# Differential attention on one core: join factors for two heads at once, and the join placed between the two sides' minima

## Chip, core and metric

The kernel runs on one core of a Trainium2 chip. The metric is the device time of one execution in microseconds (us), lower is better. The median of three executions before the change is 2317.76 us (2317.54 to 2319.17).

## What is computed

Three layers on a sequence of 1024 tokens of width 1024: a gated block with a convolution and a feed-forward part, then a layer of differential attention, then a layer of stick-breaking attention. The change touches the differential attention alone. Cut to what matters:

```python
def block(args):                       # i = 0..7, 128 query rows each
    i, qb1, qb2 = args
    mask = kpos[None, :] <= qpos[:, None]
    def probs(qb, k):
        s = jnp.einsum('bhqd,bshd->bhqs', qb, k).astype(jnp.float32) * scale
        return jax.nn.softmax(jnp.where(mask, s, -jnp.inf), axis=-1)
    a = probs(qb1, k1) - lam * probs(qb2, k2)
    return jnp.einsum('bhqs,bshe->bhqe', a.astype(v.dtype), v)
...
o = _rms(o, subln) * (1.0 - lambda_init)
o = o.reshape(b, s, DA_V) * jax.nn.silu(g)
return x + o @ w_out
```

There are 8 heads. Each has two sides (q1, k1 and q2, k2) whose softmaxes are subtracted.

## The kernel before

The program is written by hand, one instruction stream for each engine (functions `tensor`, `vector`, `scalar`, `gpsimd`, `sync`), with semaphores between them. Every engine executes its own stream strictly in order, so the order of the calls in the source is the order of the work. Small helpers at the head of the file issue every instruction, so that the profile names a helper's line: L72 is a matmul, L75 a transpose, L81 an activation, L84 a copy on ScalarE, L93 a `tensor_tensor`, L101 a `scalar_tensor_tensor`, L104 the fused minimum over a row (`tensor_tensor_reduce`), L110 a `tensor_reduce`, L113 a reciprocal.

**Groups.** `da_groups` (line 489) cuts the attention into N = 54 groups: row block 0 in two groups of 4 heads, block 1 in four groups of 2 heads, blocks 2 to 7 in eight groups of one head each. A group of block i has `width(i)` = 128 (i + 1) key columns a head. `da_first` = 22 is the first group of block 4: from there on a side has its own pair of PSUM banks, and three such pairs go round. "Five blocks", "eight blocks" are widths of 640 and 1024 columns: groups 22 to 29 have five, 30 to 37 six, 38 to 45 seven, 46 to 53 eight.

**What a group u passes through.** TensorE: `scores(u)`, both sides with the mask added, into PSUM; the banks of group u + 1 come free with the exponential of side 0 of group u. VectorE: `top(u, sides)`, the negated maximum of each row (called a minimum below), for both sides in one instruction up to group 21 and one side after the other from 22 on. ScalarE: `exp(u, 0)` and `exp(u, 1)`, which also write each row's sum. VectorE: the join. A reciprocal of side 1's sum and a small multiply with side 0's sum and lambda give a factor (both write `oss`, one column for a head), and one `scalar_tensor_tensor` over the whole width adds side 1 times its factor into side 0. TensorE: `turn_a`, transposes of the joined rows in halves of 512 columns, all through PSUM bank 6. ScalarE: `turned`, the copy of each half into one of two buffers. TensorE: the product with the values, four heads into bank 7. When four heads (a quartet) are done, ScalarE squares the bank and VectorE multiplies it with the gate (L93, 128x512) and sums the squares (L110).

**Order before.** One loop over u on each engine:

- TensorE (line 977): scores(u); transposes of u - 2, first half; product of u - 3; transposes of u - 2, second half.
- VectorE (line 1955): top(u); from group 22 on side 0, then side 1; factors and join of u - 1, which wait for exp(u - 1, 1); multiply and sum where u - 3 closes a quartet; then, in a few rounds from u = 27 to 38, pieces of other work (peaks of the gate, the factor of weight 31, the factor of the output).
- ScalarE (line 2678): exp(u, 0); copy of u - 2, second half; the square where u - 3 closes a quartet; exp(u, 1); for u = 22 to 29 the absolute sum of an eighth of weight 31 (an activation of 128x512 into OV); copy of u - 1, first half.
- GpSimd takes maxima across partitions for weights; SyncE's queue loads the weights in order. Its load of weight 31 waits for the transposes of group 3 and the join of group 2, since it overwrites their buffers.

At u = N VectorE takes the reciprocal of the norm's roots for the first four row blocks and scales them (`finish_half`, 8 times, then `finish_low`), ScalarE takes the root (`finish_root`, which needs another activation table), and TensorE transposes them (`finish_turn`) in its last round, before and behind the last product. The output projection follows.

The first exponentials are interrupted on ScalarE at u = 2 by the last two SiLU pieces, between two table loads.

Of the kernel before, what the change touches and what calls it, by code (L numbers as in the profile page):

```python
# [200 lines left out]
def block_kernel(nc, A):  # L201
    ctx = ExitStack()
    with ctx:
# [359 lines left out]
        def tensor(e):  # L563
# [413 lines left out]
            for u in range(2, N + 3):  # L977
# [4 lines left out]
                turn_a(u - 2, 0)  # L982
                if u == N + 2:
                    for i in range(4):
                        finish_turn(i, 0, i)
                if u >= 3:
                    v = u - 3
                    i, hs = da_groups[v]
                    for x, h in enumerate(hs):
                        if h % 4 == 0:  # L990
                            banks.take_at(("pva", i, h // 4), 7)
                            e.wait_ge(*banks.free(("pva", i, h // 4)))
                            e.wait_ge(*sig("bank_act").at("vv", 1, NT - 1))
                        bo = banks.ap(("pva", i, h // 4))
                        for j in range(i + 1):
                            at = width(i) * x + 128 * j
                            e.wait_ge(*sig("turned_a").at(v, at // 512))
                            mm = e.matmul(bo[:, 128 * (h % 4):128 * (h % 4) + 128], AT[v % 2][:, at:at + 128],
                                          VV[:, j, 128 * h:128 * h + 128], start=(j == 0), stop=(j == i))
                    mm.then_inc(*full.up("pva", i, hs[-1]))  # L1000
                turn_a(u - 2, 1)
                if u == N + 2:
                    for i in range(4):
                        finish_turn(i, 1, (i + 4) % 6)
# [156 lines left out]
        def vector(e):  # L1161
# [793 lines left out]
            for u in range(N + 4):  # L1955
                if u < da_first:
                    top(u, (0, 1))
                elif u < N:
                    top(u, (0,))
                    top(u, (1,))  # L1960
                if 1 <= u < N + 1:
                    v = u - 1
                    i, hs = da_groups[v]
                    w, n = width(i), len(hs)
                    a, a2 = ea(v), e2(v)
                    ri, ro = oss[:, 8 * (v % 2):8 * (v % 2) + n], oss[:, 8 * (v % 2) + 4:8 * (v % 2) + 4 + n]
                    e.wait_ge(*sig("exp").at(v, 1))
                    e.reciprocal(ri, l_sum(1, i, hs[0], n)).then_inc(*step.up())
                    e.wait_ge(*step.last())
                    e.scalar_tensor_tensor(ro, l_sum(0, i, hs[0], n), lamt[:, 5:6], ri, ALU.mult,  # L1970
                                           ALU.mult).then_inc(*step.up())
                    e.wait_ge(*step.last())
                    for x in range(n):
                        ax = a[:, w * x:w * x + w]
                        join = e.scalar_tensor_tensor(ax, a2[:, w * x:w * x + w], ro[:, x:x + 1], ax, ALU.mult, ALU.add)
                    join.then_inc(*sig("joined_a").up(v))
                if 3 <= u < N + 3 and da_groups[u - 3][1][-1] % 4 == 3:
                    i, hs = da_groups[u - 3]
# [27 lines left out]
                if u == N:  # L2006
# [174 lines left out]
        def scalar(e):  # L2181
# [496 lines left out]
            for u in range(N + 4):  # L2678
# [6 lines left out]
                turned(u - 2, 1)  # L2685
                if 3 <= u < N + 3 and da_groups[u - 3][1][-1] % 4 == 3:
                    i, hs = da_groups[u - 3]
# [15 lines left out]
                if u == 2:  # L2703
# [3 lines left out]
                    turned(0, 0)  # L2707
                if u >= 2:
                    turned(u - 1, 0)
                for x in {N + 1: range(4), N + 2: range(4, 8)}.get(u, ()):  # L2710
# [418 lines left out]
```

## Time and profile before

| | |
|---|---|
| median of three executions | 2317.76 us (2317.54 to 2319.17) |
| the profiled execution's own time | 2321.46 us |
| its span | 2319.7 us |
| TensorE busy | 2256.5 us, 97% |
| VectorE busy | 1512.9 us, 65% |
| ScalarE busy | 951.3 us, 41% |
| GpSimd busy | 202.8 us, 9% |
| granted clock of TensorE | 0.998 of full speed |
| the chain that ended last | TensorE 86%, VectorE 8%, ScalarE 4% |

The profile is one execution, and its span is what all views are measured in, from 0 to 2319.7 us. PE is TensorE, DVE VectorE, ACT ScalarE, POOL GpSimd, SP SyncE. Busy time is the time within instructions; a busy TensorE need not be at its peak. The first attention is a small part of the span, between about 1338 and 1562 us. A line's buffer names are those of the program without their numbers: PS is PSUM, RG holds the exponentials of both sides, OV and RG the transposed copies, mx the minima, oss the join's factors, R the gate.

### The profile page before, as it was taken

How to read it: one execution, taken by the hardware profiler on the slowest of the kernel's cores; microseconds unless marked ns; L12 is line 12 of the kernel's file. 1: busy time of each engine (PE TensorE's matmuls, PEld its weight loads, DVE VectorE, ACT ScalarE, POOL GpSimd, SP SyncE). 2: the span in 40 equal slices, each digit the busy share in tenths (PEclk: the TensorE clock that was granted, in tenths of full speed). 3: DMA queues.
4: the chain of work that ended last, by engine and by line, in shares of the span. 5: the costliest groups of instructions: out<-in, count | busy, mean ns of one | idle time of the engine just before them, and what ended most of it. 6: DMA issues, size and time to landing. Idle time of an engine off the chain costs nothing.

```text
span 2319.7 us, 29678 instructions
## 1 busy us (share of the span) xinstructions
PE 2256.5 (97%) x12574; PEld 1153.8 (50%) x12574; DVE 1512.9 (65%) x1959; ACT 951.3 (41%) x1396; POOL 202.8 (9%) x246
## 2 busy tenths in 40 slices
PE   7999999999999999999999988899999999999999
PEld 5455444444444444444544446664444444566655
DVE  6789857866766766778653268995553460677761
ACT  6255234423232323342332178772322321677750
POOL 0001021000000000352320200002100000000000
PEclk9999999999999999999999999999999999999999
DMA  5111110121112111112122010011032140001021
GB/s 193 37 37 37 37 37 21 53 73 70 39 37 73 62 48 70 40 39 110 37 73 73 1 37 1 1 73 63 11 104 114 51 132 1 1 1 37 2 92 55
DMA packets 51972, 120.16 MB, mean 52 GB/s; under 512 B 2890, under 2 KB 8579, under 8 KB 51456
## 3 DMA queue, kind: packets, MB, share of 16 engines
q1 hardware_dynamic: 48616, 105.40, 12.8%
q10 hardware_dynamic: 3224, 12.87, 1.6%
q8 instruction: 99, 1.62, 0.3%
q14 instruction: 33, 0.27, 0.0%
HBM read 101.49 MB, written 12.58 MB: 49 GB/s over the span
## 4 chain that ended last, share of the span: by engine, by line
PE 86%; DVE 8%; ACT 4%; DMA 1%; issue 1%; SPq 0%; DVEq 0%; ACTq 0%
PE PS L72 80%; PE PS L75 5%; ACT RG L81 2%; DVE R L93 2%; DVE R L101 1%; DVE RG L104 1%; DVE RG L101 1%; DMA RG<-in_a_w_in 1%; ACT R L81 1%; DVE oss L110 1%; DVE dg L104 1%; DVE scl L110 0%; DVE mx L110 0%; ACT OV L81 0%; DMA R<-in_x 0%
## 5 line engine op out<-in xcount | busy, mean ns | idle before, releaser
L72 PE MATMUL PS<-R,RG 128*128 128x512 f16 (+1 forms) x5568 | 1186.0, 374 | 9.2 <-DVE R L101 4.2
L72 PEld LDWEIGHTS PS<-R,RG 128*128 128x128 f16 (+1 forms) x5568 | 550.3, 103 | 637.5 <-issue 11.0
L72 PE MATMUL PS<-RG,R 128*128 128x512 f16 (+2 forms) x3080 | 601.1, 361 | 0.9 <-DVE R L93 0.5
L72 PEld LDWEIGHTS PS<-RG,R 128*128 128x128 f16 (+1 forms) x3080 | 279.3, 105 | 297.5 <-issue 15.6
L81 ACT ACTIVATE RG<-RG,scl 128x4096 f16<-128x4096 f32 (+2 forms) x70 | 177.8, 2556 | 206.8 <-DVE scl L113 206.8
L101 DVE SCALAR_TENSOR_TENSOR RG<-RG,scl 128x4096 f16<-128x4096 f32 (+2 forms) x70 | 213.0, 3050 | 71.0 <-ACT RG L81 71.0
L107 DVE TENSOR_TENSOR_SCAN RG<-RG,dg 128x128 f32<-128x128 f32 (+7 forms) x128 | 167.6, 1347 | 123.2 <-ACT RG L81 122.7
L101 DVE SCALAR_TENSOR_TENSOR R<-PS,scl,R 128x512 f32<-128x512 f32 (+1 forms) x211 | 148.5, 742 | 114.0 <-PE PS L72 107.4
L110 DVE TENSOR_REDUCE scl<-RG 128x1 f32<-128x4096 f32 (+1 forms) x35 | 150.3, 4294 | 99.8 <-DMA RG<-in_w_ff 41.2
L81 ACT ACTIVATE R<-PS,scl 128x512 f32<-128x512 f32 (+1 forms) x104 | 68.6, 686 | 265.3 <-PE PS L72 251.7
L122 POOL PARTITION_ALL_REDUCE scl<-scl x49 | 33.9, 694 | 1592.1 <-DVE scl L110 1311.2
L72 PE MATMUL PS<-R 64*128 64x512 f16 (+4 forms) x1216 | 142.7, 338 | 18.3 <-ACT RG L81 18.0
L75 PE MATMUL PS<-ident,RG 128*128 128x128 f32 x864 | 146.9, 285 | 10.1 <-DVE RG L101 7.3
L81 ACT ACTIVATE R<-R,scl 128x512 f16<-128x512 f32 (+3 forms) x68 | 79.3, 1193 | 135.4 <-DVE R L93 78.0
L101 DVE SCALAR_TENSOR_TENSOR R<-R,OV 128x1024 f32<-128x1024 f32 x104 | 129.3, 1278 | 1.0
L81 ACT ACTIVATE RG<-PS,scl 128x1024 f32<-128x1024 f32 (+4 forms) x94 | 89.0, 948 | 81.7 <-PE PS L72 81.7
L75 PEld LDWEIGHTS PS<-ident,RG 128*128 128x128 f32 x864 | 92.3, 141 | 48.4 <-issue 32.7
L81 ACT ACTIVATE RG<-PS,mx,scl 128x128 f32<-128x128 f32 (+7 forms) x128 | 106.1, 833 | 11.1 <-DVE mx L104 9.8
L93 DVE TENSOR_TENSOR R<-PS,R 128x512 f32<-128x512 f32 (+1 forms) x120 | 80.9, 685 | 44.0 <-PE PS L72 29.5
L84 ACT COPY R<-PS 128x512 f32<-128x512 f32 x72 | 40.9, 581 | 144.7 <-PE PS L75 74.2
L72 PEld LDWEIGHTS PS<-R 64*128 64x128 f16 (+1 forms) x1216 | 59.4, 99 | 79.1 <-ACT RG L81 24.8
L93 POOL TENSOR_TENSOR R<-R 128x512 f32<-128x512 f32 x56 | 86.1, 1554 | 133.2 <-ACT R L81 117.9
(141 smaller groups left out, 1675.0 us busy)
## 6 DMA issues: line engine op xcount, KB each, us to landing
RG<-in_w_ff SPq DMA_DIRECT2D x16, 2048.0 KB, 8.5
RG<-in_a_w_in SPq DMA_DIRECT2D x8, 2048.0 KB, 8.7
xspill<-R ACTq DMA_DIRECT2D x2, 4096.0 KB, 15.8
RG<-in_w_kv SPq DMA_DIRECT2D x4, 2048.0 KB, 7.9
RG<-in_b_w_in SPq DMA_DIRECT2D x4, 2048.0 KB, 8.4
RG<-in_w_in SPq DMA_DIRECT2D x3, 2048.0 KB, 8.4
R<-in_x SPq DMA_DIRECT2D x8, 512.0 KB, 8.6
RG<-in_w_out SPq DMA_DIRECT2D x2, 2048.0 KB, 7.7
```

Source lines behind the costliest of these rows:

```text
L72: return self.engine.matmul(*a, **k) if self.engine else Nothing()
L75: return self.engine.transpose(*a) if self.engine else Nothing()
L81: return self.engine.activation(*a, **k) if self.engine else Nothing()
L84: return self.engine.copy(*a) if self.engine else Nothing()
L93: return self.engine.tensor_tensor(*a) if self.engine else Nothing()
L101: return self.engine.scalar_tensor_tensor(out=out, in0=in0, scalar=scalar, in1=in1, op0=op0, op1=op1)
L104: return self.engine.tensor_tensor_reduce(*a) if self.engine else Nothing()
L107: return self.engine.tensor_tensor_scan(*a) if self.engine else Nothing()
L110: return self.engine.tensor_reduce(*a, **k) if self.engine else Nothing()
L122: return self.engine.partition_all_reduce(*a) if self.engine else Nothing()
```

## The change

On VectorE the join of group u - 1 behind both minima becomes the join of group u - 2 between the two minima (behind the one minimum up to group 21). The factors of groups with one head are computed for two groups at once, in even rounds, and wait for the second one's exponential of side 1. The transposes, the product, the square, the copies, and multiply and sum all come one round later than before, so the loops run one round longer, and the last steps move from u = N to N + 1, or from N + 2 to N + 3. ScalarE's `finish_root(0)` stays at u = N. Three dots stand for lines left out.

```diff
@@ tensor: -974,17 +974,17 @@
-            for u in range(2, N + 3):
+            for u in range(2, N + 4):
...
-                turn_a(u - 2, 0)
-                if u == N + 2:
+                turn_a(u - 3, 0)
+                if u == N + 3:
                     for i in range(4):
                         finish_turn(i, 0, i)
-                if u >= 3:
-                    v = u - 3
+                if u >= 4:
+                    v = u - 4
...
-                turn_a(u - 2, 1)
-                if u == N + 2:
+                turn_a(u - 3, 1)
+                if u == N + 3:
@@ vector: -1952,30 +1952,42 @@
-            for u in range(N + 4):
+            def join_factors(v):
+                i, hs = da_groups[v]
+                n = 2 if len(hs) == 1 else len(hs)
+                at = 8 * (v // 2 % 2 if len(hs) == 1 else v % 2)
+                ri, ro = oss[:, at:at + n], oss[:, at + 4:at + 4 + n]
+                e.wait_ge(*sig("exp").at(v + 1 if len(hs) == 1 else v, 1))
+                e.reciprocal(ri, l_sum(1, i, hs[0], n)).then_inc(*step.up())
+                e.wait_ge(*step.last())
+                e.scalar_tensor_tensor(ro, l_sum(0, i, hs[0], n), lamt[:, 5:6], ri, ALU.mult,
+                                       ALU.mult).then_inc(*step.up())
+                e.wait_ge(*step.last())
+
+            def join_sides(v):
+                i, hs = da_groups[v]
+                w = width(i)
+                a, a2 = ea(v), e2(v)
+                at = 4 + (8 * (v // 2 % 2) + v % 2 if len(hs) == 1 else 8 * (v % 2))
+                for x in range(len(hs)):
+                    ax = a[:, w * x:w * x + w]
+                    join = e.scalar_tensor_tensor(ax, a2[:, w * x:w * x + w], oss[:, at + x:at + x + 1], ax, ALU.mult,
+                                                  ALU.add)
+                join.then_inc(*sig("joined_a").up(v))
+
+            for u in range(N + 5):
                 if u < da_first:
                     top(u, (0, 1))
                 elif u < N:
                     top(u, (0,))
+                if 2 <= u < N + 2:
+                    if len(da_groups[u - 2][1]) > 1 or u % 2 == 0:
+                        join_factors(u - 2)
+                    join_sides(u - 2)
+                if da_first <= u < N:
                     top(u, (1,))
-                if 1 <= u < N + 1:
-                    v = u - 1
...
-                    e.wait_ge(*sig("exp").at(v, 1))
-                    e.reciprocal(ri, l_sum(1, i, hs[0], n)).then_inc(*step.up())
...
-                    join.then_inc(*sig("joined_a").up(v))
-                if 3 <= u < N + 3 and da_groups[u - 3][1][-1] % 4 == 3:
-                    i, hs = da_groups[u - 3]
+                if 4 <= u < N + 4 and da_groups[u - 4][1][-1] % 4 == 3:
+                    i, hs = da_groups[u - 4]
@@ vector: -2003,7 +2015,7 @@
-                if u == N:
+                if u == N + 1:
                     finish_root(0)
                     for x in range(8):
                         finish_half(x % 4, x // 4)
@@ scalar: -2675,16 +2687,16 @@
-            for u in range(N + 4):
+            for u in range(N + 5):
...
-                turned(u - 2, 1)
-                if 3 <= u < N + 3 and da_groups[u - 3][1][-1] % 4 == 3:
-                    i, hs = da_groups[u - 3]
+                turned(u - 3, 1)
+                if 4 <= u < N + 4 and da_groups[u - 4][1][-1] % 4 == 3:
+                    i, hs = da_groups[u - 4]
@@ scalar: -2704,10 +2716,9 @@
                     gate_silu(NT - 1)
                     e.wait_ge(*sig("table").at())
                     e.activation(lamt[:, 7:8], epst[:, 0:1], ACT.Exp)
-                    turned(0, 0)
                 if u >= 2:
-                    turned(u - 1, 0)
-                for x in {N + 1: range(4), N + 2: range(4, 8)}.get(u, ()):
+                    turned(u - 2, 0)
+                for x in {N + 2: range(4), N + 3: range(4, 8)}.get(u, ()):
```

## Rows read from the trace of the kernel before

**Rows 1.** Stages of 20 us: length, busy us (xcount) by engine, clock, DMA

```profile
1460.00:1480.00 20.00, 16.85 (x158) 12.73 (x157) 18.87 (x44) 14.77 (x32) 0.35 (x1) 1.00 0.00 1
```

**Rows 2.** The tiles oss and mx: ns min/median/max, first and last start

```profile
L113 DVE RECIPROCAL oss<-OV x54: 152/158/178, 1346.2 to 1546.7; 128x1 f32<-128x1 f32 x48, 128x2 f32<-128x2 f32 x4, 128x4 f32<-128x4 f32 x2
...
L81 ACT ACTIVATE RG<-PS,mx,scl x128: 447/830/1217, 1342.5 to 1545.3; 128x128 f32<-128x128 f32 x16, 128x256 f32<-128x256 f32 x16, 128x384 f32<-128x384 f32 x16, 128x512 f32<-128x512 f32 x16
```

**Rows 3.** Timeline, eight blocks, groups 47 and 48: start, us, engine, what, idle before

```profile
1514.10 1.28 DVE L104 CUSTOM_DVE_ANT_0 RG<-PS,scl 128x1024 bf16<-128x1024 f32 x1 [0.42 <-PE PS L72]
...
1515.31 1.28 DVE L104 CUSTOM_DVE_ANT_0 dg<-PS,scl 128x1024 bf16<-128x1024 f32 x1
1515.42 1.21 ACT L81 ACTIVATE RG<-PS,mx,scl 128x1024 f32<-128x1024 f32 x1 [0.24 <-DVE mx L104]
...
1516.87 1.47 PE L72 MATMUL PS<-R 64*128 64x512 f16 x12 [0.42 <-ACT RG L81]
1516.96 1.28 DVE L101 SCALAR_TENSOR_TENSOR RG<-RG,oss 128x1024 f32<-128x1024 f32 x1
...
1518.54 1.28 DVE L104 CUSTOM_DVE_ANT_0 RG<-PS,scl 128x1024 bf16<-128x1024 f32 x1 [0.29 <-PE PS L72]
```

**Rows 4.** Timeline, the same stretch, the round of group 48 behind its minima

```profile
1521.07 0.57 ACT L84 COPY OV<-PS 128x512 f32<-128x512 f32 x1
...
1521.53 0.60 ACT L81 ACTIVATE OV<-PS 128x512 f32<-128x512 f32 x1
...
1522.60 0.68 DVE L93 TENSOR_TENSOR R<-PS,R 128x512 f32<-128x512 f32 x1
...
1523.80 1.27 DVE L104 CUSTOM_DVE_ANT_0 RG<-PS,scl 128x1024 bf16<-128x1024 f32 x1
```

**Rows 5.** Timeline of VectorE: minima of side 0, six blocks, then seven

```profile
1463.51 1.01 DVE L104 CUSTOM_DVE_ANT_0 RG<-PS,scl 128x768 bf16<-128x768 f32 x1
...
1467.14 1.02 DVE L104 CUSTOM_DVE_ANT_0 RG<-PS,scl 128x768 bf16<-128x768 f32 x1 [0.22 <-PE PS L72]
...
1471.60 1.01 DVE L104 CUSTOM_DVE_ANT_0 RG<-PS,scl 128x768 bf16<-128x768 f32 x1
...
1496.57 1.15 DVE L104 CUSTOM_DVE_ANT_0 RG<-PS,scl 128x896 bf16<-128x896 f32 x1 [0.29 <-PE PS L72]
...
1500.61 1.15 DVE L104 CUSTOM_DVE_ANT_0 RG<-PS,scl 128x896 bf16<-128x896 f32 x1 [0.29 <-PE PS L72]
...
1505.47 1.14 DVE L104 CUSTOM_DVE_ANT_0 RG<-PS,scl 128x896 bf16<-128x896 f32 x1
```

**Rows 6.** Timeline, five blocks, groups 27 to 29

```profile
1431.95 0.88 DVE L104 CUSTOM_DVE_ANT_0 RG<-PS,scl 128x640 bf16<-128x640 f32 x1 [0.35 <-PE PS L72]
...
1435.25 0.88 DVE L104 CUSTOM_DVE_ANT_0 RG<-PS,scl 128x640 bf16<-128x640 f32 x1
...
1436.23 0.89 ACT L81 ACTIVATE RG<-PS,mx,scl 128x640 f32<-128x640 f32 x1
...
1438.60 0.65 ACT L81 ACTIVATE OV<-RG 128x512 f16<-128x512 f32 x1
...
1439.31 0.88 DVE L104 CUSTOM_DVE_ANT_0 RG<-PS,scl 128x640 bf16<-128x640 f32 x1
```

**Rows 7.** Timeline: TensorE's transposes of group 1, VectorE's minimum of group 4

```profile
1357.91 0.63 PE L75 MATMUL PS<-ident,RG 128*128 128x128 f32 x4 [1.71 <-ACT OV L84]
...
1362.38 1.21 DVE L110 TENSOR_REDUCE mx<-PS 128x4 f32<-128x1024 f32 x1
```

**Rows 8.** Timeline: minimum of group 53, transposes of 52, table load, transposes of 53

```profile
1542.36 1.27 DVE L104 CUSTOM_DVE_ANT_0 RG<-PS,scl 128x1024 bf16<-128x1024 f32 x1
...
1546.56 0.66 PE L75 MATMUL PS<-ident,RG 128*128 128x128 f32 x4 [2.16 <-DVE RG L101]
...
1547.86 1.28 ACT L81 ACT_TABLE_LOAD   x1
...
1550.21 0.63 PE L75 MATMUL PS<-ident,RG 128*128 128x128 f32 x4 [0.77 <-ACT OV L84]
```

More of the change, by code:

```diff
@@ L1959, in vector @@
                     top(u, (0,))
-                    top(u, (1,))
-                if 1 <= u < N + 1:
-                    v = u - 1
[L1963 to L1966, printed above, removed]
-                    e.wait_ge(*sig("exp").at(v, 1))
-                    e.reciprocal(ri, l_sum(1, i, hs[0], n)).then_inc(*step.up())
[L1969 to L1975, printed above, removed]
-                    join.then_inc(*sig("joined_a").up(v))
-                if 3 <= u < N + 3 and da_groups[u - 3][1][-1] % 4 == 3:
-                    i, hs = da_groups[u - 3]
+                if 2 <= u < N + 2:
[3 more added lines that the diff above has]
+                if da_first <= u < N:
+                    top(u, (1,))
+                if 4 <= u < N + 4 and da_groups[u - 4][1][-1] % 4 == 3:
+                    i, hs = da_groups[u - 4]
                     g = hs[-1] // 4
```

## The prediction

> **What bounds the kernel now.** I read the execution in slices of 20 us first. The first attention runs from 1338 to 1562 us of the span, and there VectorE is the fullest engine, 18.87 of 20 us, with TensorE and ScalarE well below [rows 1]. That says "VectorE bound". The next view, the single instructions, says otherwise. Call T(u) the start of group u's first minimum. With eight blocks T(u+1) - T(u) is 4.44 us, and VectorE is idle for 0.29 to 0.42 us at the end of it, waiting for the scores on TensorE; TensorE in turn waited for the exponential of side 0 [rows 3]. So the pace is a ring through three engines: minimum 1.2, exponential (it starts at T+1.32), scores (start at T+2.77, that is 1516.87 - 1514.10), next minimum 1.67 later. The exception is the round that also multiplies a finished quartet with its gate: from 1518.54 to 1523.80 is 5.26 us, with no idle time before the minimum [rows 4]. There VectorE is the bound. The ring is 3.63, 4.04 and 3.30 us for six, seven and five blocks, and the multiplying round 4.46, 4.86 and 4.06 [rows 5, 6]. Up to four blocks ScalarE (scale, two exponentials, copy, now and then a square) sets the pace, and the change leaves its instructions alone.
>
> **Factors for two heads.** A reciprocal and a small multiply run 54 times; with 24 pairs made one, 30 remain [rows 2]. Side 1's minimum starts at 1515.31 and holds the engine for 1.20 (side 0's: 1515.31 - 1514.10 = 1.21 of the printed 1.28), the join starts at 1516.96: the factors cost 0.45 us of VectorE a group [rows 3], so 24 x 0.45 = 10.8 us of its work goes. It counts only where VectorE is the bound. In even groups the factors stay, in odd groups they vanish. The pair must wait for the second head's exponential: that ends about 5.0 us after T(u-1), VectorE gets there at 4.44 + 1.2 = 5.6, so 0.6 us of slack covers it.
>
> **Where the multiply falls.** The pipeline is one group deeper, so multiply and sum (1.20 us, 1522.60 to 1523.80 [rows 4]) move from even to odd rounds, which have no factors. VectorE's work in a multiplying round of eight blocks becomes 1.21 + 1.20 + 1.20 + 1.20 = 4.81 instead of 5.26. But the multiply waits for ScalarE's square, which started 2.99 us after T and takes 0.60 [rows 4]; before, the factors covered that. I take 4.9, and 4.67 and 4.2 for seven and six blocks (each step of 128 columns is 0.13 us less for a pass, by the printed 1.28, 1.15, 1.02 and 0.88 [rows 3, 5, 6]).
>
> **The join between the minima.** Nobody waits for the older join sooner than before: the transposes of group u-3 still need a join of round u-1. What moves is side 1's minimum, later by the join (1.20) and in even rounds by 0.45 more. Behind it on ScalarE stand exponential 1, the copy, and then the next group's exponential 0, which is in the ring. Eight blocks, even round: minimum 1 ends at 1.21 + 0.45 + 1.20 + 1.20 = 4.06, exponential 1 runs 4.18 to 5.38, copy 0.48 (1521.07 to about the square at 1521.53 [rows 4]), so exponential 0 can start at 5.86, where the ring wants 4.44 + 1.32 = 5.76. The loss is 0.1 in every second round; with seven and six blocks the same sum gives 0.14 and 0.15 (an exponential is 0.11 us shorter per 128 columns: 1217 down to 447 ns over seven steps [rows 2]). If the following round multiplies, the loss disappears under it. Five blocks are different: ScalarE also takes a 0.61 us piece of the weight's absolute sum after exponential 1 (printed 0.65 [rows 6]). Minimum 1 ends at 0.81 + 0.45 + 0.80 + 0.81 = 2.87, plus 0.12 + 0.87 + 0.61 + 0.48 is 4.95; the ring wants 3.30 + 0.98 (1436.23 - 1435.25 [rows 6]) = 4.28. So each pair of rounds takes some 7.2 us instead of 6.6.
>
> **Sum of the wide groups**, T(22) to T(53), round by round as the larger of ring, VectorE's work and this ScalarE path. Five blocks: four pairs of 7.2 are 28.9 against 28.3 now, **+0.6**. Six blocks, with the extra peaks and factors of the next weight in these rounds: **-0.8**. Seven: two multiplying rounds, each 0.2 shorter, less one or two late ones at 0.14, and a factor round of VectorE alone saved nothing: **-0.4**. Eight: T(46) to T(53) holds two multiplying rounds of 5.26 now and one of 4.9 then, the other moving behind T(53): -0.36 - 0.82, plus 0.1 to 0.2 lost, **-1.0**. Three and four blocks: VectorE is relieved where ScalarE is the bound, **-0.2**; bounds 0 and -0.7 (two quartets at most 0.35 each).
>
> **The head.** Now the transpose of group 1 stands in TensorE's queue ahead of the scores of group 4, and it waits 1.71 us for ScalarE's copy, which stands behind two table loads; T(4) is 1362.4 [rows 7]. Then the scores of group 4 follow the transpose of group 0 at about 1356.2, where TensorE falls idle now, and T(4) comes near 1358.5, behind the factors and joins of group 1 on VectorE. ScalarE's exponentials and squares soon limit that lead. Carried forward through the multiplying rounds 4, 5, 7 and 9 (now 3, 4, 6 and 8) it settles at **-2.1** at group 10. Bounds: 0 if ScalarE takes it all, -3.9 if the whole lead of T(4) holds (1362.4 against 1358.5).
>
> **The drain.** One round more of transpose and product stands behind the last scores. Now the transpose of group 52 starts at T(53)+4.20, after 2.16 us of waiting for its join, and that of group 53 at T(53)+7.85; what follows is the same in both kernels [rows 8]. Afterwards, from T(53): transposes and product of groups 50 and 49 to 2.8; transposes of 51 at 3.6, behind the copy; product of 50 to 5.9; second transposes of 51 to 6.5. On ScalarE the first copy of 51 starts at 5.0, behind the last exponential, and the table load of 1.28 us with the root behind it now falls between the two copies of group 51 (before: between those of 52), so the second is at 7.2 and the transposes of 52 start at 8.0 (their join, ready at 6.9, isn't what they wait for). Product 1.8, transposes, copy: group 53 at 11.6. That is **+3.8**. Bounds: +1.7 if the table load hides (join bound), +4.5 if the copies each slip again.
>
> The load of weight 31 waits, in SP's queue, for a join and a transpose that are up to one group later, some 4.6 us; its first reader is group 22, 40 us on, so nothing. GpSimd's steps hang on none of this. The halves of the gate that VectorE finishes move behind one more join, and still end before TensorE wants them, at 13.4 against 14.3 after T(53).
>
> Total: -2.1 - 0.2 + 0.6 - 0.8 - 0.4 - 1.0 + 3.8 = **-0.1 us**. The profiled execution took 2321.46 us (span 2319.7, 1.8 around it), 3.7 above the median of 2317.76; taken off the median the same sum gives **2317.7 us**.
>
> **Rivals.** (1) *VectorE's whole saving arrives*, 10.8 us, 2307 us. For it: rows 1, and the multiplying rounds without idle time. Against it: the 0.29 to 0.42 us that VectorE waits in the plain rounds, which it would only wait longer. The Trainium skill (Perfetto Trace Analysis, "Identifying the Most-Contended Engine") says that the engine with the highest occupancy is the most contended and is to be optimized first; by that rule this case would be the one to expect. The trace speaks against it in three rounds of four. Chance 0.06. (2) *A cheap drain and no loss at five blocks*: the table load hides and the ring swallows ScalarE's piece: drain +1.7, five blocks -0.9 (two multiplying rounds 0.46 shorter), together -3.7, 2314 us. It crosses 0.2% only with a head of 3 as well. Chance 0.20. (3) *ScalarE's queue becomes the bound in all wide groups*, slower: if exponential 1 starts some 0.4 us later than I take (the order of multiply, square and minimum slips in the even rounds), every pair of six to eight blocks loses as much as the five-block ones, 0.55 us more in six pairs and 0.15 in the six that hide it under a multiply: +4.2, and with the rest near 2322; with a full drain of +4.5, 2322.5. It decides when ScalarE's exponential 0 no longer waits for a minimum (0.24 us of waiting now [rows 3], with a longer wait for the transposes before it). Chance 0.12. (4) That the pairs aren't formed is excluded: the count of the factors follows from the code.
>
> **How the numbers follow.** The forecast as it stands, within 2.5 us of no change, has 0.62. A measurement of this kernel can tell about 0.2%, 4.6 us, from no change. Faster by more: rival 1 and a good third of rival 2, with some error of my head and wide sums, 0.15. Slower by more: most of rival 3, 0.09. Within: 0.76. For the range I take the head at -3 to -1 and the drain at +1.7 to +4.5 with the wide groups 1 us either way, not all at once: 2313.5 to 2320.5.
>
> **What would show it.** Right: 30 reciprocals of the factors; T(53) 3.9 us earlier than 1542.36; multiplying rounds of about 4.9 at eight blocks and plain ones still at 4.44, with VectorE's idle time before the minimum grown in odd rounds; pairs of 7.2 at five blocks with ScalarE's exponential 0 going straight behind the copy; T(4) near 1358.5; the transposes of group 53 11.6 us after T(53), with the table load in front of a copy that TensorE waits for. Wrong: plain rounds shorter than the ring (VectorE was the bound after all), no lead at group 10, a drain that is as long as before, or exponential 0 late in every wide round.

## The result, and the profile after

The median of 13 executions after the change is 2323.69 us (2321.48 to 2324.62), against 2317.94 (2316.92 to 2320.86) for the kernel before in the same comparison: a ratio of 1.002, 95% interval 1.0012 to 1.0027. The kernel is slower by 5.75 us. The forecast was 2317.7 with a range up to 2320.5; the result lies 3.2 us above that end. The profiled execution took 2324.25 us, its span is 2322.4.

The instructions changed as the code says. In the page of the kernel after, the busy times of the engines, and in the view of the tile `oss`, its reciprocals:

```profile
PE 2259.6 (97%) x12574; PEld 1154.7 (50%) x12574; DVE 1504.1 (65%) x1911; ACT 951.1 (41%) x1396; POOL 203.1 (9%) x246
...
L113 DVE RECIPROCAL oss<-OV x30: 153/157/169, 1348.4 to 1546.1; 128x2 f32<-128x2 f32 x28, 128x4 f32<-128x4 f32 x2
```

30 reciprocals instead of 54 [rows 2], and VectorE is busy 8.8 us less (1504.1 against 1512.9), TensorE 3.1 us more with as many matmuls. So less work on VectorE, and a longer time.

To see where, I cut the attention of both traces at T(u), the start of group u's first minimum, and at the last square. The first minimum falls 2.03 us earlier in the execution after (1338.84 against 1340.87), ahead of every changed instruction, so stretches are compared and not positions. (The clock goes with it: near 116 us of the span TensorE's granted clock is at half of full speed for some 7 us in the execution before and for some 3.5 in the one after.) The last column is what the forecast's terms gave.

| stretch | before | after | difference | forecast |
|---|---|---|---|---|
| T(0) to T(14), the head | 50.86 | 49.80 | -1.06 | -2.1 |
| T(14) to T(22), three and four blocks | 22.69 | 22.57 | -0.12 | -0.2 |
| T(22) to T(30), five blocks | 28.28 | 30.82 | +2.54 | +0.6 |
| T(30) to T(38), six blocks | 32.69 | 33.43 | +0.74 | -0.8 |
| T(38) to T(46), seven blocks | 34.27 | 33.84 | -0.43 | -0.4 |
| T(46) to T(53), eight blocks | 32.70 | 31.69 | -1.01 | -1.0 |
| T(53) to the last square, the drain | 14.27 | 17.95 | +3.68 | +3.8 |
| from there to the end | 763.07 | 763.46 | +0.39 | 0 |

The sum is +4.73. Four of the forecast's seven terms stand to 0.15 us; the miss is in the five blocks (1.9), the six blocks (1.5) and the head (1.0).

**Five blocks.** The timeline of the kernel after, rounds 25 to 28, T(25) being 1422.33 (start, us, engine, what, idle before and its releaser):

```profile
1424.98 0.62 ACT L81 ACTIVATE OV<-PS 128x512 f32<-128x512 f32 x1
1425.70 0.69 DVE L93 TENSOR_TENSOR R<-PS,R 128x512 f32<-128x512 f32 x1 [0.88 <-ACT OV L81]
...
1426.90 0.88 DVE L104 CUSTOM_DVE_ANT_0 RG<-PS,scl 128x640 bf16<-128x640 f32 x1
...
1428.96 0.88 DVE L104 CUSTOM_DVE_ANT_0 dg<-PS,scl 128x640 bf16<-128x640 f32 x1
...
1429.88 0.88 ACT L81 ACTIVATE RG<-PS,mx,scl 128x640 f32<-128x640 f32 x1 [0.92 <-DVE mx L104]
...
1430.13 0.88 DVE L104 CUSTOM_DVE_ANT_0 RG<-PS,scl 128x640 bf16<-128x640 f32 x1 [0.29 <-PE PS L72]
...
1430.75 0.62 ACT L81 ACTIVATE OV<-RG 128x512 f16<-128x512 f32 x1
...
1431.37 0.57 ACT L84 COPY OV<-PS 128x512 f32<-128x512 f32 x1
...
1431.83 0.89 ACT L81 ACTIVATE RG<-PS,mx,scl 128x640 f32<-128x640 f32 x1
...
1434.15 0.88 DVE L104 CUSTOM_DVE_ANT_0 RG<-PS,scl 128x640 bf16<-128x640 f32 x1 [1.20 <-PE PS L72]
```

Round 26 is the forecast's mechanism to within 0.1 us: side 1's minimum ends 2.9 after T(26), then exponential 1, the weight's piece and the copy follow each other, and the next group's exponential 0 goes straight behind at T(26)+4.93 (forecast 4.95). Rounds 26 and 27 take 7.25 together, against 6.59 before. But the top of the fence is what was not foreseen: in the multiplying round 25, whose exponential 0 is late for the same reason, VectorE waits 0.88 us for ScalarE's square. Rounds 25 and 29 take 4.57 and 4.58, where rounds 24 and 28, with the multiply, took 4.06 before.

**Six blocks.** The kernel after, timeline around the multiplying round 33 (1453.17 to 1458.80), and then three windows of 2 us behind it (length, busy us of PE, PEld, DVE, ACT, POOL, granted clock, DMA):

```profile
1456.17 0.69 DVE L93 TENSOR_TENSOR R<-PS,R 128x512 f32<-128x512 f32 x1
...
1457.37 0.68 DVE L110 TENSOR_REDUCE scl<-R 128x1 f32<-128x512 f32 x1
1457.96 0.33 DVE L96 TENSOR_SCALAR scl<-scl 128x1 f32<-128x1 f32 x2
...
1458.33 0.16 DVE L113 RECIPROCAL scl<-scl 128x1 f32<-128x1 f32 x1
...
1461.09 2.10 PE L72 MATMUL PS<-R 64*128 64x512 f16 x12 [2.27 <-ACT RG L81]
...
1466.12 1.15 PE L72 MATMUL PS<-R 64*128 64x512 f16 x12
```
```profile
1459.00:1461.00 2.00, 0.00 (x0) 0.00 (x0) 1.93 (x5) 1.14 (x3) 0.00 (x0) 1.00 0.02 4
...
1461.00:1463.00 2.00, 1.91 (x12) 0.84 (x12) 1.75 (x4) 1.02 (x2) 0.00 (x0) 0.53 0.03 8
...
1463.00:1465.00 2.00, 2.00 (x14) 1.88 (x13) 1.55 (x3) 0.86 (x4) 0.00 (x0) 0.62 0.00 0
```

Round 33 now holds multiply, sum, a peak of the gate (1457.37) and the factor of weight 31 (1457.96 to 1458.5): 5.63 us. TensorE runs dry for 2.27 us. Behind that its granted clock is 0.53 and 0.62 of full speed, the lower of its two levels (1.2 GHz) for most of 4 us, and the same twelve score matmuls take 2.10 instead of 1.15 us. Rounds 34 and 35 take 4.65 and 4.02 (before 3.86 and 3.63). It isn't the only place; between groups 22 and 23:

```profile
1411.00:1413.00 2.00, 0.91 (x8) 0.72 (x7) 1.93 (x6) 1.02 (x3) 0.00 (x0) 1.00 0.00 0
...
1413.00:1415.00 2.00, 1.75 (x13) 0.87 (x14) 1.01 (x3) 1.05 (x5) 0.00 (x0) 0.58 0.00 0
...
1415.00:1417.00 2.00, 2.00 (x13) 2.00 (x13) 1.73 (x4) 1.41 (x5) 0.00 (x0) 0.57 0.00 0
```

**The drain.** The kernel after, timeline from T(53), which is 1540.99:

```profile
1540.99 1.28 DVE L104 CUSTOM_DVE_ANT_0 RG<-PS,scl 128x1024 bf16<-128x1024 f32 x1 [0.29 <-PE PS L72]
...
1544.44 0.63 PE L75 MATMUL PS<-ident,RG 128*128 128x128 f32 x4 [0.77 <-ACT OV L84]
...
1546.51 1.28 ACT L81 ACT_TABLE_LOAD   x1
...
1547.54 0.60 PE L75 MATMUL PS<-ident,RG 128*128 128x128 f32 x4
...
1548.17 0.58 ACT L84 COPY RG<-PS 128x512 f32<-128x512 f32 x1
...
1548.90 0.63 PE L75 MATMUL PS<-ident,RG 128*128 128x128 f32 x4 [0.77 <-ACT RG L84]
...
1552.52 0.63 PE L75 MATMUL PS<-ident,RG 128*128 128x128 f32 x4 [0.77 <-ACT OV L84]
```

The transposes of groups 52 and 53 start 7.91 and 11.53 after T(53) (forecast 8.0 and 11.6; before 4.20 and 7.85 [rows 8]). Each half of a group goes through bank 6: transpose, copy, transpose.

### The profile page after: what moved, and what is told of

Its sections match the earlier page's. It is cut to its first block, busy times and chain, and to the rows that moved or that the text cites. A ratio compares the mean times of both kernels' runs of the same rounds, so it can differ in the third digit from the quotient of the medians.

```text
span 2322.4 us, 29630 instructions
## 1 busy us (share of the span) xinstructions
PE 2259.6 (97%) x12574; PEld 1154.7 (50%) x12574; DVE 1504.1 (65%) x1911; ACT 951.1 (41%) x1396; POOL 203.1 (9%) x246
## 4 chain that ended last, share of the span: by engine, by line
PE 85%; DVE 8%; ACT 5%; DMA 1%; issue 1%; SPq 0%; DVEq 0%; ACTq 0%
PE PS L72 80%; PE PS L75 5%; ACT RG L81 3%; DVE R L93 1%; DVE R L101 1%; DVE RG L101 1%; DVE RG L104 1%; DMA RG<-in_a_w_in 1%; ACT R L81 1%; ACT OV L81 1%; DVE oss L110 1%; DVE dg L104 1%; ACT OV L84 0%; DVE scl L110 0%; DVE mx L110 0%
```

## Experiments

The first four are edits of the kernel after, and ask whether ScalarE's queue behind the join (theory) or something else makes the wide groups long.

**e1**, the weight's piece ahead of exponential 1 on ScalarE; the join stays between the minima.

```diff
-                if u < N:
-                    exp(u, 1)
                 if da_first <= u < da_first + 8:
                     ...
+                if u < N:
+                    exp(u, 1)
```

> The changed kernel, with ScalarE's piece of weight 31 (groups 22 to 29) ahead of the exponential of side 1 instead of behind it. Theory A (ScalarE's queue: the minimum of side 1 comes late, and behind its exponential stand the piece, the copy and the next group's exponential of side 0): ScalarE now waits about 1 us ahead of exponential 1, the piece fits in there, and the chain from the minimum to the next exponential 0 is 0.61 us shorter. T(22) to T(30) falls from 30.8 to about 28 us, the time by 2 to 3 us against the changed kernel (2323.7), to 2321 or so. Theory B (the deeper pipeline costs: the multiply waits for the square in odd rounds, and the drain is longer; where the join stands is neutral): T(22) to T(30) stays within 0.5 us of 30.8 and the time at 2323.7.

**e2**, the join behind both minima again.

```diff
+                if da_first <= u < N:
+                    top(u, (1,))
                 if 2 <= u < N + 2:
                     ...
                     join_sides(u - 2)
-                if da_first <= u < N:
-                    top(u, (1,))
```

> The changed kernel, with the join of u - 2 behind both minima again from group 22 on; pairs of factors and the deeper pipeline stay. Theory A: exponential 1 starts 1.2 to 1.65 us sooner, no exponential 0 is late, the rounds fall back to the ring (3.3, 3.63, 4.04, 4.44) and the multiplying ones to 3.7, 4.1, 4.5, 4.85: T(22) to T(53) from 129.8 to about 125 us (before: 127.9), the time 4 to 5 us below the changed kernel, near 2319, about 1 us above the kernel before because of the drain. Theory B: T(22) to T(53) stays near 129, the time within 1 us of 2323.7.

**e3**, the root, with its table load, a round later on ScalarE.

```diff
-                if u == N:
+                if u == N + 1:
                     finish_root(0)
```

> The changed kernel, with ScalarE's first root (and its table load) one round later, at u = N + 1, so that it falls between the copies of group 52 as in the kernel before, no longer between those of 51. If the drain's length is set by the table load ahead of a copy on which TensorE waits, the transposes of group 53 start about 10.5 us after T(53) instead of 11.5 (7.85 before), and the time falls by 1 us to about 2322.7. If the drain is the extra product and transposes alone, nothing moves (2323.7).

**e4**, e2 with the factors of one head at a time.

```diff
-                n = 2 if len(hs) == 1 else len(hs)
+                n = len(hs)
...
-                e.wait_ge(*sig("exp").at(v + 1 if len(hs) == 1 else v, 1))
+                e.wait_ge(*sig("exp").at(v, 1))
...
-                    if len(da_groups[u - 2][1]) > 1 or u % 2 == 0:
-                        join_factors(u - 2)
+                    join_factors(u - 2)
```

> As e2 (join behind both minima, deeper pipeline), but with factors for each head by itself as in the kernel before. It differs from e2 in the pairs alone. Both theories: VectorE has 0.45 us more in the multiplying rounds, which are bound by it, and nothing in the others: these rounds are 0.3 to 0.45 us longer than in e2, seven of them from T(22) to T(53), and some rounds with extra work on VectorE too: T(22) to T(53) about 3 us longer than in e2 (some 127.5 to 128), the time 2.5 to 3 us above e2. Were VectorE the bound in every round, it would be 24 x 0.45 = 10.8 us above e2; were the ring the bound in all, it would equal e2.

Measured, with stretches in us from each kernel's profile (the kernel before had a median of 2318.89 beside these; intervals are of the ratio to it):

| kernel | T(22)-T(30) | T(30)-T(38) | T(38)-T(53) | drain | median | ratio |
|---|---|---|---|---|---|---|
| after | 30.82 | 33.43 | 65.53 | 17.95 | 2323.69 | 1.0012 to 1.0027 |
| e1 | 29.03 | 32.27 | 65.57 | 17.95 | 2321.16 | 0.9999 to 1.0018 |
| e2 | 28.71 | 32.13 | 65.14 | 17.95 | 2319.54 | 0.9989 to 1.0008 |
| e3 | 30.59 | 33.31 | 65.57 | 17.95 | 2323.59 | 1.0007 to 1.0027 |
| e4 | 27.77 | 33.43 | 65.98 | 18.09 | 2320.11 | 0.9998 to 1.0017 |

The timeline of e1, in rounds 25 and 26:

```profile
1425.44 0.69 DVE L93 TENSOR_TENSOR R<-PS,R 128x512 f32<-128x512 f32 x1 [0.28 <-ACT OV L81]
...
1428.58 0.64 ACT L81 ACTIVATE OV<-RG 128x512 f16<-128x512 f32 x1
...
1429.62 0.89 ACT L81 ACTIVATE RG<-PS,mx,scl 128x640 f32<-128x640 f32 x1 [0.30 <-DVE mx L104]
...
1430.50 0.58 ACT L84 COPY OV<-PS 128x512 f32<-128x512 f32 x1
...
1430.96 0.90 ACT L81 ACTIVATE RG<-PS,mx,scl 128x640 f32<-128x640 f32 x1
```

The piece (1428.58) now lies where ScalarE waited for side 1's minimum, and VectorE's wait for the square falls from 0.88 to 0.28. The five blocks get 1.8 us back, and with the join behind 2.1. So ScalarE's queue it was, and the piece is most of it; the join alone still costs some 0.3 there. From group 38 on it costs 0.4 us over 15 rounds (65.53 against 65.14), no more than the 0.1 a pair that the forecast had. But it shows in the multiplying rounds 41 and 49 too (4.67 and 5.00, in e2 4.55 and 4.90), where the forecast let it disappear.

In the six blocks e1 gains 1.2, though nothing differs there that the theory names. Round 33 lasts 5.63 in both, and the windows of e1 behind its idle time say the rest:

```profile
1457.00:1459.00 2.00, 0.36 (x4) 0.12 (x2) 1.62 (x6) 0.60 (x1) 0.00 (x0) 1.00 0.01 4
1459.00:1461.00 2.00, 1.37 (x16) 0.88 (x17) 2.00 (x4) 1.02 (x4) 0.00 (x0) 1.00 0.00 0
1461.00:1463.00 2.00, 2.00 (x18) 1.76 (x16) 2.00 (x4) 2.00 (x4) 0.00 (x0) 1.00 0.00 0
```

The clock stays at 1.00, and rounds 34 and 35 take 3.87 and 3.63: 7.50 instead of 8.67. The fall of the clock behind round 33 is worth 1.2 us. e3 and e4 have it there (33.31 and 33.43), e1 and e2 don't. e1's edit takes nothing away from round 33, so that this profile has no fall is no merit of the edit.

e3 settles the drain. Its timeline:

```profile
1548.16 0.59 ACT L84 COPY RG<-PS 128x512 f32<-128x512 f32 x1 [1.68 <-PE PS L75]
...
1548.89 0.63 PE L75 MATMUL PS<-ident,RG 128*128 128x128 f32 x4 [0.77 <-ACT RG L84]
...
1550.15 1.28 ACT L81 ACT_TABLE_LOAD   x1
...
1552.51 0.63 PE L75 MATMUL PS<-ident,RG 128*128 128x128 f32 x4 [0.77 <-ACT OV L84]
```

The table load has gone from between the copies of group 51, and the copy starts at the same place (1548.16), now with 1.68 us of waiting for the transposes. The drain is 17.95 to the hundredth. The load wasn't what set it.

e4 against e2 has 24 reciprocals more (54), and is 1.2 us longer from T(22) to T(53) (127.18 against 125.98), with one fall of the clock in this stretch in each, in other places. Some 3 us had been expected. I took no price of the pairs from that, since e4 had rounds 22 and 23 at 3.23 and 3.29 where e2 had 3.99 and 3.76. That raised a question of its own: does the pair's wait for the second exponential cost something at the step to five blocks? The next four ask it, and mend what the first had shown.

**e5**, the extra peaks and factors moved out of rounds 31 to 38.

```diff
-                if da_first + 9 <= u < da_first + 13:
+                if u in (da_first + 9, da_first + 13, da_first + 17, da_first + 21):
...
-                if u == da_first + 16:
+                if u == da_first + 25:
                     finish_factor()
-                if u == da_first + 11:
+                if u == da_first + 29:
                     factor(31)
```

> The changed kernel, with VectorE's extra work (four peaks of the gate in groups 31 to 34, the factor of weight 31 in 33, the output's factor in 38) moved to odd rounds without a multiply (31, 35, 39, 43, 47, 51). Theory: the deeper pipeline brought the multiply into round 33, where a peak and the weight's factor already stand; that round took 5.63 us, left TensorE idle for 2.27 us, and in some executions its granted clock fell to 0.5 behind that idle time (about 1.1 us more in rounds 34 and 35). Round 33 should now take 4.2 to 4.3 us, T(30) to T(38) fall from 33.4 (32.3 without the clock's fall) to about 30.9, no idle time of TensorE there be over 1.5 us, the granted clock stay at 1.00, and the time be 2 to 3 us below the changed kernel, near 2321.5. Rival (the extras only move, and cost their 0.6 us wherever they stand): T(30) to T(38) near 32.3 and the sum over all groups unchanged but for the clock.

**e6**, e2 with pairs from group 24 on alone.

```diff
+                pair = v >= da_first + 2
-                n = 2 if len(hs) == 1 else len(hs)
+                n = 2 if pair else len(hs)
...
-                    if len(da_groups[u - 2][1]) > 1 or u % 2 == 0:
+                    if u - 2 < da_first + 2 or u % 2 == 0:
```

> As e2 (join behind both minima), but the factors are paired from group 24 on only. In e2 rounds 22 and 23 took 3.99 and 3.76 us, with single factors (e4) 3.23 and 3.29. Theory (the pair's wait for the second head's exponential, where ScalarE is still behind from the narrow groups, is what costs): round 22 falls to about 3.25 and round 23 to 3.3, T(22) to T(30) from 28.7 to 27.5, the time 1.2 us below e2. Rival (it is the wider PSUM of the first five-block groups, not the wait): nothing moves.

**e7**, e2 with the second halves of the last three groups through PSUM bank 4.

```diff
-                    b = banks.take_at(("ta", v, s), 6)
+                    b = banks.take_at(("ta", v, s), 4 if s and v >= N - 3 else 6)
```

> As e2, but the second transposed half of the last three groups goes to PSUM bank 4 instead of bank 6. In every kernel so far a group costs 3.62 us at the end (transposes, copy, transposes, copy in turn through one bank), whichever way ScalarE's root stands (e3 moved it for nothing). Theory (the drain is set by this ping-pong through bank 6): a group costs about 2.8 us, the stretch from T(53) to the last square falls from 17.95 to 16 us or so, the time by 1.5 to 2 us against e2. Rival (the drain is set by TensorE's own work or the late multiply): under 0.5 us.

**e8**, the edits of e5, e6 and e7 together.

> All of it: join behind both minima, pairs from group 24 on, the extras of e5 and the tail bank of e7. If the three costs add up, T(22) to T(53) is about 122 us (e2: 126.0) and T(53) to the last square about 16 (17.95): some 6 us below e2 (2319.5) at most, 2314 to 2315 us, 4 us below the kernel before. If VectorE's relief only lengthens its waits, it stays near 2317.

The kernel before had a median of 2318.62 beside these.

| kernel | T(22)-T(30) | T(30)-T(38) | T(38)-T(53) | drain | median | ratio |
|---|---|---|---|---|---|---|
| e5 | 30.84 | 30.67 | 65.36 | 17.95 | 2320.30 | 0.9998 to 1.0017 |
| e6 | 28.68 | 31.77 | 65.12 | 17.95 | 2318.34 | 0.9990 to 1.0008 |
| e7 | 28.43 | 32.12 | 65.11 | 16.04 | 2318.03 | 0.9989 to 1.0007 |
| e8 | 27.62 | 30.25 | 65.01 | 16.04 | 2315.04 | 0.9976 to 0.9993 |

e5: the six blocks fall from 33.43 to 30.67, round 33 from 5.63 to 4.35, and the fall of the clock is gone with it. Of the 2.76 us some 1.2 is that fall and the rest the extra work, of which only 0.15 comes back, in round 35 (3.78 against 3.63 in e1): from T(38) on e5 is no longer than the kernel after.

e6 speaks against my guess on the pairs: with single factors rounds 22 and 23 still take 3.82 and 3.76. What sets these two rounds is the clock. With a fall there they take 7.47 to 7.84 together (e1, e2, e3, e5, e6, e7, e10), without one 6.52 or 6.53 (e4, e8, and e11 below, which has pairs there). e6 and e8 run the same instructions up to there, and give the clock's price once more. TensorE's scores of group 23 in e6 and in e8:

```profile
1411.83 1.53 PE L72 MATMUL PS<-R 64*128 64x512 f16 x12 [1.34 <-ACT RG L81]
```
```profile
1413.47 0.99 PE L72 MATMUL PS<-R 64*128 64x512 f16 x12 [1.34 <-ACT RG L81]
```

And the windows of e6, then of e8, in which these lie:

```profile
1412.00:1414.00 2.00, 2.00 (x17) 1.31 (x14) 0.98 (x2) 1.16 (x4) 0.00 (x0) 0.53 0.00 0
```
```profile
1412.00:1414.00 2.00, 0.66 (x8) 0.35 (x8) 1.93 (x7) 1.65 (x4) 0.00 (x0) 1.00 0.00 0
1414.00:1416.00 2.00, 2.00 (x24) 1.62 (x19) 1.58 (x4) 1.64 (x6) 0.00 (x0) 1.00 0.00 0
```

The same idle time of 1.34 us ahead, the same matmuls, and once the clock falls and once it doesn't. Rounds 22 and 23 take 7.58 with the fall and 6.53 without: 1.05 us. Two more couples of kernels have the same instructions there: e10 and e4 (7.54 and 6.52) and, with the join between the minima, e1 and e11 (7.84 and 6.53). So the price is 1.0 to 1.3 us.

e7: the drain goes from 17.95 to 16.04. Its transposes:

```profile
1545.52 1.04 PE L75 MATMUL PS<-ident,RG 128*128 128x128 f32 x8
...
1548.18 1.04 PE L75 MATMUL PS<-ident,RG 128*128 128x128 f32 x8
```

All eight transposes of a group run at once, and a group takes 2.66 us instead of 3.62 (1552.52 - 1548.90 in the kernel after). So the drain is the exchange of transposes and copies over one bank. The Trainium skill (Perfetto Trace Analysis, "Matmuls") says to let independent groups rotate through different PSUM banks, so that one is emptied while the next is filled; the trace agrees, at 0.96 us a group.

The last three ask how much of e8 belongs to the change at all.

**e9**, the kernel before with the edits of e5 and e7. 

> The kernel before, with e8's two additions alone: the extras moved to rounds 31, 35, 39, 43, 47, 51 (which are rounds without a multiply here too) and the tail bank. If the pairs and the deeper pipeline are worth something by themselves, this stays above e8: rounds with a multiply at 4.06 to 5.26 us as before, T(22) to T(53) about 126 us (127.9 less the extras' 2), T(53) to the last square 14.27 less 0.8, the time 2.5 to 3 us below the kernel before, some 2315.5 to 2316, against 2315.0 of e8. If they are worth nothing, it is at or below e8.

**e10**, e4 with the edits of e5 and e7: as e8, without pairs. 

> e8 with factors for each head by itself: it differs in the pairs alone. The relief of 24 x 0.45 = 10.8 us of VectorE reaches the time only in the rounds with a multiply (4.06, 4.46 to 4.50, 4.85, 5.26 instead of 3.91 to 4.06, 4.20, 4.55, 4.90): seven of them from T(22) to T(53), 0.1 to 0.36 each. T(22) to T(53) about 1.5 us above e8's 122.9, the time 1 to 2 us above 2315.0. If the pair's wait costs as much as it saves, it equals e8.

**e11**, e1 with the edits of e5 and e7: the join between the minima, pairs everywhere. 

> The changed kernel with the join between the minima kept, ScalarE's piece ahead of exponential 1 (e1), the extras moved (e5) and the tail bank (e7). The join between the minima should then cost only what is left of ScalarE's queue: 0.1 us in rounds 37, 41, 43, 49 and 51 and some tenths in rounds 25 to 29. T(22) to T(53) 0.7 to 1.2 us above e8's 122.9 (plus about 1 us where the granted clock falls in rounds 22 and 23, as in five of the profiles so far), the time near 2316.

The kernel before had a median of 2317.95 beside these.

| kernel | T(22)-T(30) | T(30)-T(38) | T(38)-T(53) | drain | median | ratio |
|---|---|---|---|---|---|---|
| e9 | 28.28 | 31.38 | 67.89 | 13.30 | 2317.36 | 0.9990 to 1.0009 |
| e10 | 28.79 | 31.09 | 66.63 | 16.18 | 2318.99 | 0.9990 to 1.0007 |
| e11 | 27.72 | 30.68 | 65.40 | 16.03 | 2315.88 | 0.9977 to 0.9994 |

e9: the edits around the change give the kernel before 0.4 us from T(22) to T(53) and 1.0 in the drain, and no difference in the median that can be told. The expectation missed: T(22) to T(53) was to take about 126 us, and took 127.55. The extra work that left rounds 31 to 38 (31.38 against 32.69) comes back in rounds 39, 43, 47 and 51 (4.27, 4.50, 4.75 and 4.56, where the ring takes 4.04 and 4.44), since each of these rounds still has factors of its own. In e5 it found odd rounds without factors. e8 needs 122.88 us from T(22) to T(53), 4.7 less than e9, and pays 2.7 for it in the drain. So depth and pairs are worth some 2 us, once the rest is mended (2.3 by the medians of these two kernels, 2317.36 and 2315.04, taken in different comparisons). e8 and e11 are the only kernels here that are faster than the kernel before by more than the interval, by 3.6 and 2.1 us.

e10 against e8 is the price of the pairs: 126.51 against 122.88, 3.6 us, of which some 1.0 is a fall of the clock in e10 (rounds 22 and 23 at 7.54, in e8 6.53). The other 2.6 stand against 13 factor computations fewer in this stretch (18 reciprocals of factors instead of 31), 5.85 us of VectorE's work at 0.45 each. Less than half arrives: 1.5 us in the multiplying rounds, as expected, and 1.1 in the odd rounds that hold the moved extra work (round 43 takes 4.50 with factors and 4.04 without), which I had not counted. Depth alone, without pairs, gains nothing that can be told: e10's median is 1.6 us above e9's in the same comparison, and the intervals lie on each other. Pairs at the old depth I didn't build.

e11 against e8: with the join between the minima (and pairs from the start) the stretch is 0.9 us longer, and the kernel beats the one before all the same. So the place of the join costs under 1 us, once ScalarE's piece no longer stands behind it.

## Why the prediction was wrong

**The step that failed** is "If the following round multiplies, the loss disappears under it". I took a multiplying round as VectorE's work, with slack for ScalarE. But the square comes behind exponential 0 and a copy on ScalarE, so a late exponential 0 makes it late too, and the multiply waits (0.88 us in round 25). The loss adds to the multiply. The pair of rounds without a multiply came out as worked out (7.25); the two with one, 24 and 25, and 28 and 29, took 7.87 and 7.88 instead of 7.2. That is 1.35 of the 1.9 us missed at five blocks. The other 0.6 is in rounds 22 and 23 (7.82), where the clock fell, at a price of 1.0 to 1.3; what they would have taken in this kernel without the fall no run shows (6.53 in e11, with the piece moved).

**A second step failed** beside it: the sum takes TensorE's speed as given in every term, and has nothing for its clock. In the kernel after the granted clock fell in four places behind T(0), in three of them at a cost: in rounds 22 and 23, behind round 33 (1.2) and, most likely, behind the attention (below). That is over 2 us of the 4.7.

**Six blocks**, forecast -0.8, came out at +0.74. 1.2 of the 1.5 missed is the fall of the clock behind round 33, which my sum had no term for, although it gathered the work into that round. The other 0.3 can't be laid to one round, since the forecast gives this stretch as one number. The multiplying rounds took 4.35 (round 37, and round 33 where e5 takes its extra work away) where 4.2 was forecast, which would make up for it. The extra work in round 33 would not: it costs 1.28 us there (5.63 against 4.35), and before it cost as much in two rounds (5.04 and 4.34 against 4.46 and 3.63).

**Seven and eight blocks**: -0.43 and -1.01 against -0.4 and -1.0. In the kernel after the multiplying rounds take 4.67 (forecast 4.67) and 5.00 (4.9), the plain ones 4.43, with VectorE's idle time grown in the odd round:

```profile
1517.32 1.21 ACT L81 ACTIVATE RG<-PS,mx,scl 128x1024 f32<-128x1024 f32 x1 [0.60 <-DVE mx L104]
...
1518.17 1.28 DVE L104 CUSTOM_DVE_ANT_0 RG<-PS,scl 128x1024 bf16<-128x1024 f32 x1 [0.88 <-PE PS L72]
```

The ring through three engines holds as forecast; the saved factors turn into waiting.

**The head**, forecast -2.1, came out at -1.06. Counted from T(0), T(4) was 3.06 us earlier than before, where the forecast had 3.9 (1362.4 against 1358.5); from there to T(10) 2.0 of the lead went, where the forecast let 1.8 go. So most of the miss stands at T(4) already. In the kernel after, that minimum follows at once behind the factors and the join of round 3 on VectorE, and these factors hold an instruction of 1.08 us where others of its kind take 0.22; the trace before has it in the same round, ahead of a T(4) that comes 4 us after it ended. First the row of the kernel before, then that of the kernel after:

```profile
1357.13 1.09 DVE L101 SCALAR_TENSOR_TENSOR oss<-OV,lamt,oss 128x2 f32<-128x2 f32 x1
```
```profile
1355.12 1.08 DVE L101 SCALAR_TENSOR_TENSOR oss<-OV,lamt,oss 128x4 f32<-128x4 f32 x1
```

Its 0.86 us above the usual match the 0.8 missed; no run took it away, and why it takes so long isn't shown. The clock has a part in the head too: all eleven kernels with the deeper pipeline have a fall there. Where it lies in round 4 (kernel after, e1, e2) the head is 49.80 to 49.83; where it lies in rounds 6 and 7 (the other eight) 50.29 to 50.43.

**The drain**: the size was right (+3.68 against +3.8), the cause wrong. Not the table load between two copies but bank 6 sets the pace; the load lay beside it by chance. The bound of +1.7 "if the table load hides" was therefore no bound: e3 hid it and gained nothing.

**Rivals.** The whole saving (2307 us) is out: even in the best surroundings less than half arrives. The Trainium skill's rule that the engine with the highest occupancy is to be optimized first (Perfetto Trace Analysis, "Identifying the Most-Contended Engine") is borne out here only in part: with the pairs alone changed (e8 against e10), 2.6 of 5.85 us arrived, and in the kernel after VectorE lost 8.8 us of busy time while the time rose by 5.75. Rival 3, ScalarE's queue as the bound in all wide groups, named 2322 to 2322.5, close to the time measured; but seven and eight blocks, for which it stood, came out as forecast, so that the nearness is luck. It was ScalarE's queue, at five blocks alone, together with the clock. My own bounds on the wide groups (1 us either way) were too narrow for a rule, round by round, that had never been seen with both losses in one round.

**What stays open.** The parts say 4.7 us (profiles) and the medians 5.75. The 0.39 in the rest of the span goes with another fall of the clock, in the kernel after at 1655 us (windows of 2 us):

```profile
1655.00:1657.00 2.00, 1.30 (x4) 0.33 (x5) 2.00 (x4) 0.89 (x2) 0.09 (x1) 0.67 0.01 4
1657.00:1659.00 2.00, 2.00 (x6) 0.56 (x6) 1.85 (x3) 0.62 (x1) 0.00 (x0) 0.50 0.00 0
```

The three kernels with a fall there (after, e2, e4) take 763.46 to 763.75 us from the last square to the end, the ten others 762.85 to 763.15. The place of T(0) goes with the clock near 116 us: without a fall there it is 1336.8 to 1337.6 (e2, e5, e6, e9), with one 1338.5 to 1339.1, with one twice as long 1340.0 to 1340.9 (among them the kernel before, whose profiled execution was 3.7 us above its median). Why the clock falls behind some idle times and not behind others wasn't settled. How often it falls in executions that weren't profiled is in part on record, as each one's mean granted clock: 0.996 or 0.997 in all 13 of the kernel after, 0.999 in 18 of the 31 of the kernel before beside e1 to e4. So the kernel after loses more to its clock in nearly every execution, and not in the profiled one alone. e1's gain of 2.5 us is in part luck: among executions with a mean of 0.997 its median is 1.7 us below that of the kernel after, among those with 0.996 it is 0.8 below.

## What to carry to other kernels

Before work is moved within one engine's stream, follow the *next* engine's queue through the round that is already the longest: a late instruction delays everything in order behind it, and the loss adds where the engine that receives it has no slack. Work saved on the fullest engine arrived here only in rounds where that engine did not wait at the end; count those rounds first. A deeper pipeline shifts which rounds coincide, and costs a round of transpose and copy at the end, so side work has to move along with it (e5), and the drain wants its own PSUM banks (e7). Let a profile of the changed kernel show the granted clock too: here over 2 us of the loss was neither work nor waiting, but matmuls at the lower clock.

## What the runs showed of the hardware

In the attention TensorE's granted clock fell to its lower level for 3 to 4 us in places where the kernel before kept 1.00, always behind idle times of TensorE: 1.33 or 1.34 us between groups 22 and 23 (eight of the eleven kernels with the deeper pipeline: the kernel after, e1, e2, e3, e5, e6, e7, e10), 2.0 to 2.3 behind round 33 (kernel after, e3, e4), and in the head 1.94 to 1.96 (kernel after, e1, e2), or two shorter ones, 1.00 and 0.94, close together (the other eight). A fall cost 1.0 to 1.3 us where TensorE was in the ring, about 0.5 in rounds 6 and 7, and nothing in round 4 (4.67 with it, 4.68 without). It isn't a matter of the length alone: between groups 22 and 23 1.33 us in e4 and e11 and 1.34 in e8, behind round 33 2.27 in e1, and 1.71 and 2.16 in the kernel before [rows 7, 8] had no fall behind them. A kernel whose TensorE runs dry at a busy place risks a second loss of about the size of the first, and two profiles that differ by a microsecond may differ in this alone.
